# Head norms of the mixer: the sums of squares as eight 512-column matmuls into one 8-row tile, three of them in the last recurrence

## The chip, the cores and the metric

The kernel runs on one core of one Trainium2 chip, as one launch. The metric is the time of one execution on the device, in microseconds (us): the median of three runs. One further execution is recorded by the profiler, and all rows in this document come from such records.

## The reference, cut to what matters

The program is a decoder trunk of two layers on 512 tokens. A layer begins with a "mixer": four heads of differential attention and four heads of a gated delta rule (a recurrence over chunks of 64 tokens). Each head gives a vector of 128 numbers for each token. Each of the eight vectors is normalized on its own, and the recurrent ones are multiplied by a gate:

```
o = rms_norm(o, subln_g) * (1.0 - lam_init)                     # attention, each head over its 128 numbers
o = rms_norm(o, norm_g) * jax.nn.silu(z.reshape(...))           # delta rule, each head over its 128 numbers
h = h + jnp.concatenate([o_da, o_gdn], axis=-1) @ w_out[i]
```

with `rms_norm(x, g) = x * rsqrt(mean(x * x) + 1e-6) * g`. The product with `w_out` (1024 x 1024) follows, then a mixture of experts, which is much the larger part of the layer.

## The kernel before, in words

Everything lies transposed: features on the 128 partitions, tokens along the columns. `mixt` is [128, 8, 512]: eight heads (0 to 3 attention, 4 to 7 delta rule), 128 features on the partitions, 512 tokens. Each engine has its own instruction stream written out by hand, and the streams meet at counted semaphores. An engine runs its stream in order.

The mixer. `mixer` runs for t = 0 to 3 (128 tokens each, two chunks of 64) thirteen steps k. Steps 0 to 8 invert the chunk matrices (`invert`, L1122), steps 9 to 12 are the recurrence (`recur`), and in every step `attend` puts a piece of the attention of head t, so that both fill each other's gaps. In the recurrence, for chunk c = 2t and c = 2t + 1: `values_of(c)` (PE, L1204) multiplies the state; VectorE subtracts it from `u_sb` (`new_values`, L1655, which gives semaphore step_vn); `state_of(c)` (PE, L1213, 4 products of 128 columns) makes the update, which VectorE adds to the state (`new_state`, L1661); `output_of(c)` (PE, L1224 and L1225, 8 products of 64 columns) makes the output of the chunk, which ScalarE copies to `mixt` (L699). ScalarE copies the transposed w to `pw` (L691) before the first `values_of` of a t. In the attention, unit u is one block of 128 queries: scores (L1038), exponentials on ScalarE (L705), weights on VectorE (L1575 to L1584), `turn(u)` (transposes on PE, L1046), the copy `turned(u)` on ScalarE (L718), `weighted(u)` (PE, L1055), and for a whole head the copy `head_out` to `mixt` (L711).

The norms, after the mixer. ScalarE squares the eight heads into `sq_mix` (L448). PE sums over the partitions with the squares as the stationary operand and one column of ones as the moving one: `norm_sums`, 8 heads x 4 token blocks = 32 products of one column (L408), into 32 columns of bank 4. ScalarE takes the roots (L439), VectorE the reciprocals (L444), and PE spreads each over 128 partitions again (`norm_spread`, L432, 4 products of 128 columns for each head, into banks 5 and 6 in turn). VectorE scales head by head (L1702), then multiplies heads 4 to 7 by the gate `gzt` (L1707), and ScalarE and VectorE split the result into `act_hi` (L770) and `act_lo` (L452), which the product with `w_out` takes (`slab_product`, L385 to L387: three products of 512 columns for each of 8 input blocks, and so for each of 8 output slabs; its first slab waits for each `act_lo` block). The matrices here are plain fp32 except in `slab_product`, where they are fp32r (one pass). The profile records each plain fp32 product as two MATMUL records.

PE's own line for this tail:

```
mixer(invert, recur, attend)
weighted(H * NT - 1)
pe.wait_ge(S["at_oc"], H)
norm_sums(pe, "mix", 2 * H, sq_mix)
norm_spread(pe, "mix", 2 * H)
```

## Time and profile before

| | us |
|---|---|
| median of three runs (lowest, highest) | 3712.5 (3712.1, 3715.87) |
| profiled execution, its own time | 3716.72 |
| its span, first to last instruction | 3714.9 |

PE is busy for 95% of the span, VectorE for 75%, ScalarE for 41%, GpSimd for 34%. The stage of this change stands in the span twice, once in each layer: from 387.3 to 417.0 us and from 2230.7 to 2260.3 us. To read it one wants the chain of work that ended last in that stretch, the waits, and TensorE's granted clock, which has two levels here: 1.00 (2.4 GHz) and 0.50 (1.2 GHz).

### The profile page before, as it was taken

What the parts mean: (1) busy time and instruction counts of PE and PEld (TensorE: products, weight loads), DVE (VectorE), ACT (ScalarE), POOL (GpSimd) and SP (SyncE); (2) the same over time, 40 slices, a digit from 0 to 9 for tenths busy, and PEclk for the clock granted to TensorE, in tenths of its full rate; (3) what the DMA queues carried; (4) which work ended last, traced back from release to release, by engine and by line L of the source; (5) the groups of instructions that cost most, each with busy time, mean ns of one, the idle gap of its engine ahead of it and who ended that gap; (6) DMA issues with size and microseconds to landing.
All of it is one profiled execution on the core that took longest, in us unless ns stands there. A gap on an engine that the chain in (4) does not pass through costs nothing.

```text
span 3714.9 us, 60532 instructions
## 1 busy us (share of the span) xinstructions
PE 3515.7 (95%) x20002; PEld 3316.9 (89%) x20002; DVE 2780.4 (75%) x5764; ACT 1522.7 (41%) x2306; POOL 1276.7 (34%) x1052
## 2 busy tenths in 40 slices
PE   7999999999998999999899899999999989999997
PEld 5877899999998999999778778999999989999996
DVE  6257478898886888888562664888988878888884
ACT  4334333336664333333333433333476633333333
POOL 0000001218774456665000000022277744565640
PEclk9999799999999999999999988999999999999998
DMA  3200144448889999999222002444588899999981
GB/s 131 80 24 1 46 139 147 145 161 291 299 298 354 370 368 375 371 380 359 92 76 80 7 1 68 139 145 148 179 291 301 298 355 383 367 377 371 367 325 61
DMA packets 266273, 814.24 MB, mean 219 GB/s; under 512 B 24816, under 2 KB 106992, under 8 KB 262512
## 3 DMA queue, kind: packets, MB, share of 16 engines
q1 hardware_dynamic: 92592, 339.05, 25.3%
q0 software_dynamic: 73728, 268.47, 19.2%
q10 hardware_dynamic: 99776, 204.50, 15.4%
q8 instruction: 94, 1.54, 0.2%
q14 instruction: 83, 0.68, 0.1%
HBM read 709.16 MB, written 102.76 MB: 219 GB/s over the span
## 4 chain that ended last, share of the span: by engine, by line
PE 63%; DMA 18%; DVE 10%; issue 5%; POOL 3%; ACT 1%; DVEq 1%; SPq 0%; ACTq 0%; POOLq 0%; PEldq 0%
PE bank L385 16%; PE bank L386 16%; PE bank L387 16%; DMA gath<-slabs,rows_of 10%; DMA gath<-u_rows,rows_of 6%; PE bank L1342 5%; POOL gath L537 2%; PE bank L1122 2%; DVE acc L1982 2%; PE bank L408 2%; DVE wlo L382 1%; PE bank L432 1%; DVE act_w L1943 1%; PE bank L1298 1%; PE bank L1225 1%
## 5 line engine op out<-in xcount | busy, mean ns | idle before, releaser
L382 DVE TENSOR_TENSOR wlo<-raw,whi 128x1024 fp32r<-128x1024 f32 x636 | 803.1, 1263 | 410.1 <-ACT whi L375 377.8
L385 PE MATMUL bank<-act_hi,whi 128*128 128x384 f32 (+1 forms) x2944 | 1054.2, 358 | 22.0 <-DVE act_lo L452 13.7
L386 PE MATMUL bank<-act_lo,whi 128*128 128x384 f32 (+1 forms) x2944 | 1040.7, 354 | 0.0
L387 PE MATMUL bank<-act_hi,wlo 128*128 128x384 f32 (+1 forms) x2944 | 1040.3, 353 | 0.0
L375 ACT ACTIVATE whi<-raw 128x1024 fp32r<-128x1024 f32 x636 | 674.9, 1062 | 500.8 <-PE bank L387 460.0
L385 PE MATMUL bank<-w_hi,whi 128*128 128x384 f32 x2048 | 698.6, 341 | 54.9 <-DVE w_lo L1948 54.7
L386 PE MATMUL bank<-w_lo,whi 128*128 128x384 f32 x2048 | 692.9, 338 | 0.0
L387 PE MATMUL bank<-w_hi,wlo 128*128 128x384 f32 x2048 | 692.6, 338 | 0.0
L529 POOL TENSOR_TENSOR onehot<-onehot,cidx 128x800 f32<-128x800 f32 x56 | 124.0, 2244 | 1547.9 <-DVEq L1833 1547.9
L385 PEld LDWEIGHTS bank<-act_hi,whi 128*128 128x128 f32 x2944 | 558.3, 190 | 64.2 <-issue 13.4
L537 POOL DMA_INDIRECT gath<-slabs,rows_of x256 | 489.1, 1910 | 298.8 <-DVE acc L1982 257.5
L387 PEld LDWEIGHTS bank<-act_hi,wlo 128*128 128x128 f32 x2944 | 557.5, 189 | 36.4
L386 PEld LDWEIGHTS bank<-act_lo,whi 128*128 128x128 f32 x2944 | 558.5, 190 | 34.9
L537 POOL DMA_INDIRECT gath<-u_rows,rows_of x256 | 349.6, 1366 | 459.9 <-DVE gath L1916 348.9
L385 PEld LDWEIGHTS bank<-w_hi,whi 128*128 128x128 f32 x2048 | 391.2, 191 | 65.5 <-issue 65.0
L1982 DVE SCALAR_TENSOR_TENSOR acc<-gath,hi_spare,acc 128x1024 f32<-128x1024 f32 x256 | 324.5, 1280 | 106.5 <-DMA gath<-slabs,rows_of 106.3
L386 PEld LDWEIGHTS bank<-w_lo,whi 128*128 128x128 f32 x2048 | 391.8, 191 | 0.0
L387 PEld LDWEIGHTS bank<-w_hi,wlo 128*128 128x128 f32 x2048 | 391.1, 191 | 0.0
L811 ACT ACTIVATE hst<-bank 128x384 f32<-128x384 f32 x256 | 125.6, 491 | 586.7 <-PE bank L387 568.7
L1916 DVE SCALAR_TENSOR_TENSOR gath<-gath,lo_spare 128x1024 f32<-128x1024 f32 x256 | 309.1, 1218 | 60.8 <-DMA gath<-u_rows,rows_of 59.6
L897 ACT ACTIVATE w_hi<-act_w 128x384 fp32r<-128x384 f32 x256 | 133.1, 520 | 310.6 <-DVE act_w L1943 308.7
L553 POOL TENSOR_SCALAR hot<-consts,n_cols 128x128 f32<-128x128 f32 x288 | 226.1, 793 | 0.0
(293 smaller groups left out, 3862.8 us busy)
## 6 DMA issues: line engine op xcount, KB each, us to landing
raw<-slabs SPq DMA_DIRECT2D x636, 512.0 KB
hidden_dram<-hst ACTq DMA_DIRECT2D x256, 192.0 KB
gates_dram<-stage ACTq DMA_DIRECT2D x24, 2048.0 KB
h_sb<-hidden_dram ACTq DMA_DIRECT2D x64, 768.0 KB
g_sb<-gates_dram ACTq DMA_DIRECT2D x32, 1536.0 KB
gath<-u_rows,rows_of POOLq DMA_INDIRECT x256
gath<-slabs,rows_of POOLq DMA_INDIRECT x256
res<-x_t SPq DMA_DIRECT2D x1, 2048.0 KB, 9.1
```

What stands on the lines that cost most here:

```text
L375: nc.scalar.activation(whi[k][:], raw[k][:], ACT.Copy).then_inc(s_slab_hi, 1)
L382: nc.vector.tensor_tensor(wlo[k][:], raw[k][:], whi[k][:].bitcast(F32), ALU.subtract).then_inc(s_slab_lo, 1)
L385: nc.tensor.matmul(out, a_hi, b_hi, start=first, stop=False)
L386: nc.tensor.matmul(out, a_hi, b_lo, start=False, stop=False)
L387: return nc.tensor.matmul(out, a_lo, b_hi, start=False, stop=last)
L537: nc.gpsimd.indirect_dma_start(gath[n % GR][:].rearrange("p k c -> p (k c)"), None, table, bass.IndirectOffsetOnAxis(ap=rows_of[:, n // P, ...
L553: last = nc.gpsimd.tensor_scalar(hot1[b % 2][:, tok, :], iota, n1_cols[b % 2][:, tok:tok + 1], None, ALU.is_equal)
L811: nc.scalar.activation(hst[k][:], bank[2 + k % 2][:, 0:TD], ACT.Gelu).then_inc(S["u_gelu"], 1)
L897: nc.scalar.activation(w_hi[r][:], act_w[r % 2][:, 0:TD], ACT.Copy).then_inc(S["w_hi_ready"], 1)
L1342: last = nc.tensor.matmul(heads(4 + i % 4)[:, s, :], hot1[b % 2][:, tok, :], hot2[b % 2][:, tok, :], start=True, stop=True)
L1916: V.scalar_tensor_tensor(gath[r][:], gath[r][:], 1.0, x_nat, ALU.mult, ALU.mult, accum_out=col).then_inc(S["gath_used"], 1)
L1982: V.scalar_tensor_tensor(acc[r % 2][:], gath[r][:], col, acc[r % 2][:], ALU.mult, ALU.add).then_inc(S["gath_used"], 1)
```

## The change

1. The sums. A new function `mix_sums` turns the operands round: the stationary operand is a slice of 8 columns of the constants with a one in column g and zeros elsewhere, the moving operand are the 512 columns of a head's squares. Head g's sums land in row g of one [8, 512] tile in bank 2, and the eight products add up in it (32 one-column products before, 8 of 512 columns now).
2. Their places. The sums of attention heads 0, 1 and 2 are issued by PE in the last recurrence (t = 3, steps 9, 10, 11); those of heads 4 to 7 and of head 3 after `weighted(15)`. ScalarE squares heads 0, 1, 2 in steps 6, 7, 8, head 4 in step 12, heads 5 to 7 and head 3 at the end, into parts of tiles no longer needed (`daq`, `gqt`, `dak`).
3. The roots. ScalarE takes them on the [8, 512] tile into `std8`, PE turns that with four small transposes to [128, 32], and VectorE's reciprocal reads it from PSUM.
4. The gates. VectorE multiplies heads 4 to 7 by the gate before the scaling, as soon as their squares are taken, not behind it.
5. In the last t, `state_of` and `new_state` of the last chunk are left out (nobody reads that state); `output_of` gets the wait for step_vn for itself.
6. `warm(n)`: n products of 256 columns (fp32r) into bank 7, which nobody reads, on PE while it waits: 6 behind the sums, 4 behind the transposes, 10 behind the spread.

The diff, in the order `mix_sums`, ScalarE's stream (to the roots), PE's (from `k == 9` on), VectorE's (last piece):

```diff
+        def mix_sums(pe, first, last):
+            for i in range(first, last):
+                pe.wait_ge(S["sq_ready"], sq_seen("mix") + i + 1)
+                g = MIX_ORDER[i]
+                done = nc.tensor.matmul(bank[2][0:2 * H, :], consts[:, C_HOT + 7 - g:C_HOT + 15 - g], sq_mix[i],
+                                        start=i == 0, stop=i == 2 * H - 1)
+            if last == 2 * H:
+                done.then_inc(S["ss_ready"], 1)
...
                 def attend(t, k):
                     u = NT * t
                     last = t == NT - 1
+                    if last and k in (6, 7, 8):
+                        act.wait_ge(S["at_oc"], k - 5)
+                        mix_square(k - 6)
...
                     elif k == 12:
+                        if last:
+                            act.wait_ge(S["og_copied"], 2 * NT)
+                            mix_square(3)
                         turned(u + 3 if last else u + 2)
...
                 mixer(invert, recur, attend)
+                for i in range(4, 7):
+                    mix_square(i)
                 head_out(H - 1)
-
                 act.wait_ge(S["at_oc"], H)
-                act.wait_ge(S["og_copied"], 2 * NT)
-                act.wait_ge(S["step_state"], 2 * NT)
-                act_squares(act, mixt, 2 * H, sq_mix)
-                norm_std(act, "mix", 2 * H, 1.0 / P)
+                mix_square(2 * H - 1)
+                act.wait_ge(S["ss_ready"], nth("mix") + 1)
+                nc.scalar.activation(std8[:], bank[2][0:2 * H, :], ACT.Sqrt, bias=eps_col[0:2 * H],
+                                     scale=1.0 / P).then_inc(S["std_ready"], 1)
...
                     elif k == 9:
                         turn(u + 1)
+                        if last:
+                            mix_sums(pe, 0, 1)
                     elif k == 10 and last:
                         scores_of(u + 3)
                         weighted(u + 1)
+                        mix_sums(pe, 1, 2)
                     elif k == 11:
                         if last:
                             turn(u + 2)
+                            mix_sums(pe, 2, 3)
...
                     else:
-                        state_of(2 * t + 1)
+                        if more:
+                            state_of(2 * t + 1)
                         output_of(2 * t + 1)
...
                 weighted(H * NT - 1)
+                mix_sums(pe, 3, 2 * H)
...
+                def warm(n):
+                    for i in range(n):
+                        nc.tensor.matmul(bank[7][:, 0:2 * P], whi[S_OUT % RING][:, 0, :],
+                                         whi[S_OUT % RING][:, 2:4, :], start=True, stop=True)
+                pe.wait_ge(s_slab_hi, S_OUT + 1)
+                warm(6)
+                pe.wait_ge(S["std_ready"], nth("mix") + 1)
                 pe.wait_ge(S["at_oc"], H)
-                norm_sums(pe, "mix", 2 * H, sq_mix)
+                for t in range(NT):
+                    last = nc.tensor.transpose(bank[4][:, 8 * t:8 * t + 8], std8[:, t * P:(t + 1) * P],
+                                               ident[0:2 * H, 0:2 * H])
+                last.then_inc(S["std_turned"], 1)
+                warm(4)
                 norm_spread(pe, "mix", 2 * H)
+                warm(10)
...
-                norm_rs(dve, "mix", 2 * H)
+                for j in range(H):
+                    dve.wait_ge(S["sq_ready"], sq_seen("mix") + 3 + j + 1)
+                    V.tensor_tensor(mixt[:, H + j, :], mixt[:, H + j, :], gzt[:, j, :], ALU.mult).then_inc(S["mix_z"], 1)
+                dve.wait_ge(S["std_turned"], 1)
+                V.reciprocal(rs[:, 0:2 * H * NT], bank[4][:, 0:2 * H * NT]).then_inc(S["rs_ready"], 1)
```

PE's stream in steps 11 and 12 of the last t, before (L1046 is `turn(14)`, L1213 `state_of(7)`, L1224 and L1225 `output_of(7)`, L1055 `weighted(14)`; the numbers behind the names tell buffers apart):

```order
L1225 MATMUL bank3<-intra1_115,u_sb_113 128x64
L1046 MATMUL bank5<-consts_50,at_w_100 128x128 x3
L1213 MATMUL bank7<-u_sb_113,kdec1_110 128x128 x4
L1224 MATMUL bank3<-qdec1_112,state1_98 128x64
```

and now (L1252, L1068, L1251 are the same three lines, L446 is `mix_sums`):

```order
L1252 MATMUL bank3<-intra1_115,u_sb_113 128x64
L1068 MATMUL bank5<-consts_50,at_w_100 128x128 x3
L446 MATMUL bank2<-daq_80,consts_50 8x512
L1251 MATMUL bank3<-qdec1_112,state1_98 128x64
```

The product of the last state update has gone and the sum of head 2 stands in its place. PE's stream from `weighted(15)` to the first product with `w_out`, before:

```order
L1055 MATMUL bank4<-at_wt_101,v_nat_73 128x128 x4
L408 MATMUL bank4<-consts_50,sq_mix_116 128x1 x32
L432 MATMUL bank5<-consts_50,rs_53 128x128 x4
```

and now (L1077 is `weighted(15)`, L1292 `warm`, L1299 the transposes of the roots, L436 the spread, L389 the first product):

```order
L1077 MATMUL bank4<-at_wt_101,v_nat_73 128x128 x4
L446 MATMUL bank2<-gqt_77,consts_50 8x512 x4
L446 MATMUL bank2<-dak_81,consts_50 8x512
L1292 MATMUL bank7<-whi0_59 128x256 x6
L1299 MATMUL bank4<-consts_50,std8_116 128x8 x4
L1292 MATMUL bank7<-whi0_59 128x256 x4
L436 MATMUL bank5<-consts_50,rs_53 128x128 x4
```

The 32 one-column products have become five of 512 columns here, and ten unread ones and four transposes stand between them and the spread. ScalarE's stream in steps 6 to 9 of the last t, now (L719 exponentials of unit 13, L674 the scaling of `kdec`, L737 a square, L705 the copy of w to `pw2`, which in the kernel before stands right behind `kdec`):

```order
L737 ACTIVATE daq_80<-mixt_76 128x512
L719 ACTIVATE at_s_99,at_c_102<-at_s_99,at_c_102 128x256 x2
L674 ACTIVATE kdec1_110<-kn_nat_71,gsm_84 128x128 x4
L737 ACTIVATE daq_80<-mixt_76 128x512 x2
L705 ACTIVATE pw2_75<-bank7 128x512
```

One square stands ahead of the exponentials and two ahead of the copy on which the recurrence's first product waits.

## Rows read from the trace of the kernel before

**Rows 1.** The page: the span, and busy time by engine.

```profile
span 3714.9 us, 60532 instructions
PE 3515.7 (95%) x20002; PEld 3316.9 (89%) x20002; DVE 2780.4 (75%) x5764; ACT 1522.7 (41%) x2306; POOL 1276.7 (34%) x1052
```

**Rows 2.** The chain that ended last, layer 1: start us, us, what.

```profile
384.54 2.09 PE bank L1055 x8
386.65 0.60 ACT mixt L711
...
388.06 13.80 PE bank L408 x64
401.88 0.29 ACT cols L439
402.20 0.36 DVE rs L444
402.61 10.50 PE bank L432 x64
...
413.79 2.49 DVE mixt L1707 x4
416.28 0.61 DVE act_lo L452
...
417.03 0.77 PE bank L385
```

**Rows 3.** Windows of layer 1: us, engines' busy us (records), PE clock, DMA share, GB/s.

```profile
99.00:104.00 5.00, 5.00 (x23) 1.87 (x22) 3.88 (x5) 1.96 (x3) 0.00 (x0) 1.00 0.28 105
370.90:373.80 2.90, 2.90 (x18) 2.36 (x17) 2.77 (x6) 0.00 (x0) 0.00 (x0) 1.00 0.00 0
374.10:381.30 7.20, 7.20 (x27) 5.77 (x25) 3.57 (x11) 2.19 (x6) 0.00 (x0) 0.50 0.00 1
388.00:400.00 12.00, 11.95 (x57) 11.98 (x57) 0.00 (x0) 4.83 (x8) 0.00 (x0) 0.50 0.01 1
408.30:413.00 4.70, 4.70 (x40) 4.46 (x38) 3.57 (x5) 1.26 (x2) 0.00 (x0) 1.00 0.00 0
415.10:417.00 1.90, 0.00 (x0) 0.00 (x1) 1.90 (x4) 1.90 (x5) 0.00 (x0) 0.50 0.00 0
417.00:421.50 4.50, 4.47 (x11) 3.53 (x12) 4.50 (x8) 0.89 (x1) 0.00 (x0) 0.50 0.01 4
```

**Rows 4.** Timeline, PE: start us, us, engine, line, form, count [idle before].

```profile
98.93 0.40 PE L386 MATMUL bank<-act_lo,wba_hi 128*8 128x512 f32 x1
363.02 1.06 PE L1122 MATMUL bank<-inv_b,kbg 128*128 128x128 f32 x8
370.88 0.43 PE L1224 MATMUL bank<-qdec,state 128*128 128x64 f32 x2
374.42 2.08 PE L1213 MATMUL bank<-u_sb,kdec 64*128 64x128 f32 x8
377.66 0.69 PE L1224 MATMUL bank<-qdec,state 128*128 128x64 f32 x2
2260.32 0.47 PE L385 MATMUL bank<-act_hi,whi 128*128 128x512 f32 x1 [3.94 <-DVE act_lo L452]
```

**Rows 5.** Timeline, ScalarE and VectorE: start us, us, engine, line, form [idle before].

```profile
364.12 0.60 ACT L691 ACTIVATE pw<-bank 128x512 f32<-128x512 f32 x1 [0.34 <-PE bank L1122]
387.28 4.26 ACT L448 ACTIVATE sq_mix<-mixt 128x512 f32<-128x512 f32 x8
402.20 0.35 DVE L444 RECIPROCAL rs<-cols 128x32 f32<-128x32 f32 x1 [22.97 <-ACT cols L439]
404.72 0.75 DVE L1702 SCALAR_TENSOR_TENSOR mixt<-mixt,lam,bank 128x512 f32<-128x512 f32 x1 [2.17 <-PE bank L432]
413.13 0.75 DVE L1702 SCALAR_TENSOR_TENSOR mixt<-mixt,par,bank 128x512 f32<-128x512 f32 x1 [0.24 <-PE bank L432]
```

**Rows 6.** One line's instructions, both layers: duration ns (min, median, max).

```profile
L1002 PE MATMUL bank<-consts,ba_t x8: 202/202/223, 126.1 to 1963.5; 8*128 8x8 f32 x8
```

More of the change, by code:

```diff
@@ L96 @@
 C_EPS = C_POS + NC
-NCONST = C_EPS + 2
+C_HOT = C_EPS + 2
+NCONST = C_HOT + 16
 Q_MIX, Q_FFN, Q_PLE, Q_FIN = 0, 8, 16, 24
@@ L224, in trunk @@
         m3 = [gates_at + (16 * 16 + 80) * 4]
-        sq_mix = place("sq_mix", [P, 2 * H, T], F32, m3)
+        std8 = place("std8", [2 * H, T], F32, m3)
+        sq_mix = [daq[:, 0, :], daq[:, 1, :], daq[:, 2, :], gqt[:, 0, :], gqt[:, 1, :], gqt[:, 2, :], gqt[:, 3, :],
+                  dak[:, 0, :]]
+        MIX_ORDER = (0, 1, 2, H, H + 1, H + 2, H + 3, 3)
         m = [arena]
@@ L333, in trunk @@
             rhs_ready kdec_ready qdec_ready uw_ready uw_copied step_v step_vn step_s step_o step_state og_copied state_zero
-            mix_scaled mix_z mix_ready wout_added q_hi_ready q_lo_ready rstd_copied qt_scaled wq_evac subk_ready
+            mix_z std_turned wout_added q_hi_ready q_lo_ready rstd_copied qt_scaled wq_evac subk_ready
             score_ready score_read tk_dve tk_act selt_ready selt_copied
@@ L719, in turned, with mix_square @@
                                          ACT.Copy).then_inc(S["at_trc"], 1)
+                def mix_square(i):
+                    nc.scalar.activation(sq_mix[i], mixt[:, MIX_ORDER[i], :], ACT.Square).then_inc(S["sq_ready"], 1)
                 def attend(t, k):
@@ L1219, in output_of @@
                         pe.wait_ge(S["qdec_ready"], t + 1)
+                        pe.wait_ge(S["step_vn"], c + 1)
                         if c > 0:
@@ L1682, in recur @@
                             setup(t + 1, "pow_n")
-                        new_state(2 * t + 1)
+                        if more:
+                            new_state(2 * t + 1)
                 setup(0, "arg_t")
@@ L1696, in _ @@
                 mixer(invert, recur, attend)
-                norm_rs(dve, "mix", 2 * H)
+                for j in range(H):
[3 more added lines that the diff above has]
+                V.reciprocal(rs[:, 0:2 * H * NT], bank[4][:, 0:2 * H * NT]).then_inc(S["rs_ready"], 1)
                 for j in range(2 * H):
                     dve.wait_ge(S["rstd_bc"], bc_seen("mix") + j + 1)
+                    if j >= H:
+                        dve.wait_ge(S["mix_z"], j - H + 1)
                     gain = lam[:, 70:71] if j < H else par[:, Q_GDN:Q_GDN + 1]
@@ L1703, in _ @@
                     i.then_inc(S["norm_used"], 1)
-                for j in range(2 * H):
-                    dve.wait_ge(S["norm_used"], used_seen("mix") + j + 1)
-                    if j >= H:
-                        V.tensor_tensor(mixt[:, j, :], mixt[:, j, :], gzt[:, j - H, :], ALU.mult).then_inc(S["mix_ready"], 1)
                 act_low(dve, mixt, KD)
@@ L2068, in constants @@
     c[:, C_EPS] = EPS
+    c[:, C_HOT + 7] = 1
     return c
```

5 lines of the change are left out of this document (1 added, 4 removed).

## The prediction

> **What bounds the kernel now.** I looked first at the page: PE is busy for 95% of the span [rows 1]. A busy PE can still be a PE with nothing useful to do, so the second view was the chain of work that ended last, in the stretch of the norms. There the steps stand one behind the other with no cover: `weighted(15)` 2.09 us, the copy of head 3, the 32 one-column products 13.80 us, the roots, the reciprocals, the spread 10.50 us, the gates 2.49 us, the first `act_lo`, the first product with `w_out` at 417.03 us [rows 2]. From the end of the copy to that product it is 29.8 us, twice in the span. Nobody works beside it: VectorE has been idle for 22.97 us when it takes the reciprocals [rows 5], and the DMA engines are at 0.00 to 0.01 [rows 3]. So what is saved here is saved in full, as long as the next stage is bound by PE. The third view, windows with the granted clock, says at what clock this runs: 0.50 from 374.1 us through the whole sums, 1.00 in the second half of the spread, then 0.50 again for the first products (11 records in 4.5 us) [rows 3]. Half of the stage's length is the clock.
>
> **What the clock follows.** While `output_of(6)` ran (370.9 to 373.8 us), PE was busy for 2.90 of 2.90 us at 1.00, and then the clock fell [rows 3]. Those are products of 64 columns. Under one-column products it stayed at 0.50 for 12 us of a PE that was busy throughout; under the 512-column products it came back after 4.5 us. From about 98.9 us on 24 products have a stationary operand of 8 columns only and 512 moving ones (one of them stands in [rows 4]); they lie in a stretch at 1.00, 23 records in 5.00 us [rows 3]. [...]
>
> **The price of a new sum.** No plain fp32 product of 128 rows and 512 columns is in the trace. From one side: four fp32 products of 128 columns are 8 records in 1.06 us at 1.00 [rows 4], of which the last record's tail is about 0.2, so 0.21 us each; four times the columns give 0.86 us, and 1.71 us at 0.50. From the other side: two records at the pace of the 8-column products, 0.22 us, would be 0.43 us. I take 0.86, since the 128-column rows are plain fp32 as the new sums are and those 8-column ones are not.
>
> **The walk, at the times of layer 1.** I follow the streams from 361 us with the durations of before and full clock.
> - ScalarE: a square costs 4.26 / 8 = 0.53 us [rows 5]. One lands ahead of the exponentials of unit 13 (a gap of 0.3 us takes most, 0.15 late), two between `kdec` and the copy of w. That copy starts at 364.9 instead of 364.12 [rows 5], and the recurrence's first product with it: 0.75 us late.
> - PE: the sum of head 0 stands ahead of `state_of(6)`, which waited for VectorE anyway; that makes 0.97 late. The sum of head 1 stands ahead of `values_of(7)`, which waited too: 1.08 late, at 371.0. `output_of(6)` takes 2.9 us (0.365 for each of 8 pairs of records, from its 0.43 rows with their tails), `turn(14)` 0.3, the sum of head 2 0.86; `state_of(7)` is gone (2.0 us at half clock [rows 4]). `output_of(7)` starts at 376.0.
> - From here before ran at 0.50. At 1.00: `output_of(7)` 2.9 us instead of 4.9 (0.62 a pair, the 0.69 rows), `weighted(14)` 0.64, `turn(15)` 0.43, the copy 0.60 and two hand-overs; the weights of unit 15 are no longer behind `new_state(7)` on VectorE and are there in time. `weighted(15)` starts at 380.9 instead of 384.54 and streams for 0.86 us. The squares of heads 4 to 6 (ScalarE, from 380.8) and 3 (after its copy, done at 383.5) stay ahead of the sums that need them. Five sums, 4.3 us and a tail of 0.15: done at 386.2, where before it was 401.86 [rows 2].
> - Roots: 512 columns from PSUM are the 0.60 us of the head copy [rows 2] where 32 columns were 0.29; `warm(6)` (6 x 0.11) ends before them. The four transposes have a twin, the transposes of `ba_t` with the same 8 rows, 202 ns each and overlapped [rows 6]: 0.4 us and a hand-over. Reciprocal 0.35, with `warm(4)` beside it. The spread starts at 387.7 instead of 402.61.
> - First scaling 1.2 us behind that at 1.00 (2.11 at 0.50 [rows 2, 5]), the last one seven steps of 1.0 us later (that is PE's pace at 1.00: 40 records in 4.70 us, 8 a head [rows 3]): 395.8 instead of 413.13.
> - The gates (2.49 us) have moved to where VectorE was idle. They cost nothing while that idle time is there (from 402.20 - 22.97 = 379.2 us on [rows 5]; in the walk 8 us are left of it); without it, 2.5 us. `act_lo` follows the last scaling after 0.7 us, the first product 0.83 us later: 397.35 instead of 417.03. That is 19.7 us.
> - The first products: 11 records at 0.43 instead of 0.22 us in layer 1 [rows 3], 2.2 us; 8 in layer 2 (started at 2260.32 [rows 4] with the clock still up, which fell and came back), 1.6 us. `warm(10)`, 1.1 us, fills the 1.7 us between the spread and them, so the clock has no reason to fall, and it delays nothing.
>
> Sum: 19.7 + 2.2 = 21.9 us in layer 1, 19.7 + 1.6 = 21.3 in layer 2, whose start stands in the same place of its stage: 43.2 us if the clock holds all the way.
>
> **What the clock takes back.** It may not. `output_of(7)` is again 2.9 us of 64-column products, now between the sum of head 2 and `weighted(14)`, and the same stretch with the same neighbours fell in one place and not in the other in this very trace: where in it the chip looks decides. A fall at about 381 us, behind `output_of(7)`, would make `weighted(15)` and three of the five sums run at half clock: 0.86 + 3 x 0.86, about 3.4 us. I take one such fall in the two layers: 43.2 - 3.4 = 39.8 us. Against the profiled execution (3716.72 us, its span and 1.8 us around it) that is 3676.9; that execution is 4.2 us above the median, which the position of the clock's falls explains as well as anything, so from the median 3712.5 I expect **3672.7 us**.
>
> The Trainium skill, in "TensorE: Matmul & The Clock Gate", section "HAM oscillation — how this bites in real kernels", puts the loss of the clock down to idle gaps of PE between bursts of products. The trace disagrees: the fall at 374 us came out of 2.90 us of unbroken work. By the page's rule there is no fall at all after the change, and the sum would be 43.2 us.
>
> **The rivals.**
> 1. The clock holds in both layers: 43.2 us, 3669.3. For it: there are 2.6 us of 512-column work more in the recurrence, and the page's rule above. Against: the fall out of a busy PE. Chance 0.28.
> 2. It falls early in both, as before at 374 us. Then `output_of(6)`'s end, the sum of head 2 and everything to `weighted(15)` run at 0.50, the sums begin at 387.4 at 0.50 and bring the clock back after 3.7 us: done at 393.7, 7.5 us later than in the walk. Gain 14.4 + 13.8 = 28.2 us, 3684.3. For it: same place, same products. Against: two sums more right around them. Chance 0.2.
> 3. The clock doesn't come back under the sums either. Five at 1.71 us: done at 396.1, `warm(6)` and `warm(4)` (0.21 each now) delay the rest by about 1 us, the spread starts 3.8 us earlier than before and runs as before; with the gates gone 2.4 us more, and up to 2.2 for the first products. 6.2 to 8.4 us a layer, 14.6 in all: 3697.9. Against it: the stretch from 99 us at 1.00. Chance 0.09.
> 4. The time is given back behind the stage, by slabs that arrive late: within 7 us of before, 3709. The DMA engines are idle here and four slabs lie ready; nothing speaks for it. Chance 0.04.
> 5. Slower: a 512-column sum costs much more than 0.86 us, for instance because fp32 squares can't be streamed at that pace. Eight of them stand on the path in each layer; the gain of 21.6 us is gone when each costs 2.7 us more, 3.6 in all. At 4 us each it would be 8 x 3.15 - 21.6 = 3.6 us a layer, 3719.7. Against: no fp32 row has a pace above 0.21 us for 128 columns. Chance 0.03.
>
> My forecast, one or a few short falls, 36 to 41 us: 0.36.
>
> **The numbers.** Rival 1 to rival 2 is 3669 to 3684, which holds 0.84. The unknown costs (the roots, hand-overs, the sum from 0.43 us up: eight sums at 0.43 less would be 3.4 us a layer) and the spread of a few us by the clock's falls elsewhere widen that to 3665 to 3689. What a measurement of this kernel tells from no change is about 0.2%, 7.4 us: faster by more than that 0.93 (all but rivals 4 and 5), the same 0.04, slower 0.03.
>
> **What would show it.** In the changed profile: two records of about 0.43 us for each sum at 1.00; PE's sums done about 5.3 us behind the start of `weighted(15)`; VectorE's idle time ahead of the reciprocals under 5 us; the spread at 1.00 from its first record; the first product 9.7 us behind the start of the spread, and its records at 0.22 us from the first on; the stage (start of the head copy to first product) about 15 us instead of 30.4. Wrong would be: sums at 1.71 us, a spread at 0.50 (rival 3), a clock of 0.50 from 374 us on (rival 2), or a PE that waits for slabs in the first products (rival 4).

## The result, and the profile after

| | before | after |
|---|---|---|
| median, us (lowest to highest), 4 executions each | 3712.3 (3700.56 to 3715.87) | 3657.25 (3654.71 to 3662.85) |
| profiled execution: its time, its span | 3716.72, 3714.9 | 3655.65, 3653.8 |

The ratio is 0.9869, 95% interval 0.9849 to 0.9889: 55 us faster. The forecast was 3672.7, its range began at 3665.0, so the change gave more than the range allowed. A second comparison of the same two kernels gave 0.9855 (0.9824 to 0.9885).

The page of the changed kernel, for [rows 1]:

```profile
span 3653.8 us, 60398 instructions
PE 3480.2 (95%) x19938; PEld 3274.3 (90%) x19938; DVE 2780.2 (76%) x5756; ACT 1522.4 (42%) x2306; POOL 1285.0 (35%) x1052
```

PE (TensorE's matmuls) has a share of 95% in both; it was busy for 35.5 us less, but the page does not say where in the span the 61 us went. The chain that ended last in layer 1 does, for [rows 2] (start us, us, what):

```profile
384.63 0.61 ACT at_wt L732
...
385.27 2.07 PE bank L1077 x8
387.35 5.81 PE bank L446 x10
393.16 0.91 PE bank L1292 x6
394.07 0.35 PE bank L1299 x4
394.41 0.67 PE bank L1292 x4
395.08 7.84 PE bank L436 x64
...
402.95 0.75 DVE mixt L1752
403.69 0.61 DVE act_lo L466
...
404.44 0.47 PE bank L389
```

The 13.80 us of one-column sums are 5.81 us now (five of the eight sums; the other three lie in the recurrence), and ScalarE's copy of head 3 is off the chain, since PE has other heads' sums to do meanwhile. The spread takes 7.84 us where it took 10.50. The gates (2.49 us) are gone from between the last scaling and the first `act_lo`. The windows with the granted clock, for [rows 3]:

```profile
375.40:378.30 2.90, 2.90 (x17) 2.37 (x16) 2.84 (x5) 0.00 (x0) 0.00 (x0) 1.00 0.00 0
379.80:382.70 2.90, 2.90 (x18) 2.36 (x17) 1.56 (x4) 1.01 (x4) 0.00 (x0) 1.00 0.00 0
384.00:390.70 6.70, 6.01 (x16) 2.57 (x15) 2.45 (x4) 4.66 (x7) 0.00 (x0) 0.54 0.01 2
391.00:394.00 3.00, 3.00 (x13) 1.05 (x10) 0.00 (x0) 0.68 (x1) 0.00 (x0) 1.00 0.00 0
394.90:400.80 5.90, 5.90 (x50) 5.54 (x48) 3.74 (x5) 2.52 (x4) 0.00 (x0) 1.00 0.00 1
405.00:411.00 6.00, 6.00 (x28) 4.95 (x27) 5.34 (x8) 1.04 (x2) 0.00 (x0) 1.00 0.03 8
```

Both `output_of` pass at 1.00; then the clock falls for 6.8 us (383.35 to 390.17 us by the trace's clock record), over the end of `weighted(14)`, `turn(15)`, `weighted(15)` and the first one and a half of the last five sums, and is back at 1.00 before the sums end. Spread and first products are at 1.00 throughout. The same in PE's timeline, for [rows 4]:

```profile
369.91 1.03 PE L446 MATMUL bank<-daq,consts 128*8 128x512 f32 x2
370.87 1.04 PE L1239 MATMUL bank<-u_sb,kdec 64*128 64x128 f32 x7
...
385.27 2.07 PE L1077 MATMUL bank<-at_wt,v_nat 128*128 128x128 f32 x8 [0.69 <-ACT at_wt L732]
387.28 5.02 PE L446 MATMUL bank<-gqt,consts 128*8 128x512 f32 x8
392.13 1.02 PE L446 MATMUL bank<-dak,consts 128*8 128x512 f32 x2
...
394.00 0.42 PE L1299 MATMUL bank<-consts,std 8*128 8x8 f32 x4
```

A sum is two records and takes 370.87 - 369.91 = 0.96 us at full clock, which is close to the 1.06 us, tail included, of the four fp32 products with 128 standing and 128 moving columns in [rows 4]: the same number of moving columns in all. ScalarE and VectorE, for [rows 5]:

```profile
393.19 0.68 ACT L788 ACTIVATE std<-bank,consts 8x512 f32<-8x512 f32 x1 [3.25 <-PE bank L446]
383.86 0.69 DVE L1744 TENSOR_TENSOR mixt<-mixt,gzt 128x512 f32<-128x512 f32 x1 [1.35 <-ACT gqt L737]
385.77 1.90 DVE L1744 TENSOR_TENSOR mixt<-mixt,gzt 128x512 f32<-128x512 f32 x3 [1.22 <-ACT gqt L737]
394.45 0.36 DVE L1746 RECIPROCAL rs<-bank 128x32 f32<-128x32 f32 x1 [6.78 <-PE bank L1299]
```

The gates lie where VectorE idled, and 6.78 us of that idle time are left.

**The stage measured as a whole.** From the start of the last copy of w to the first addition of the product with `w_out`, read in the same way from every trace (a0 and a1 are runs told of below; "half" is the time at clock 0.50 within it):

```
us                     w copy->   head copy  spread->   product->  whole   half
                       head copy  ->spread   product    addition
before        layer 1    22.54      15.95      14.42      8.02     60.93   41.0
before        layer 2    22.62      15.95      14.34      7.39     60.30   37.5
after         layer 1    19.49       7.53       9.52      5.77     42.32    6.8
after         layer 2    19.46       7.55       9.53      5.72     42.26    6.8
a0 (again)    layer 1    18.24       5.90       9.52      5.76     39.42    0
```

So the stage gave 18.6 and 18.0 us, 36.6 in all. These two traces are typical: in the 16 layers of the eight kernels that have the old stage (before, b0 to b4, d1, d2) it took 57.4 to 61.1 us, 59.7 in the mean; in the six layers of after, a0 and a6 it took 39.4 to 42.3, 41.3 in the mean. That is 36.8 us for two layers. The two spans differ by 61.1 us. Of the other 24.5 most lies where the diff changes no instruction: the expert stages, from the first to the last `w_hi` of a layer, took 572.1 and 575.7 us before and 566.1 and 564.2 after, 17.5 us less. The experiments follow both leads.

### The profile page after: what moved, and what is told of

It is laid out like the page before. It is cut to its first block, busy times and chain, and to the rows that moved or that the text cites. A ratio compares the mean times of both kernels' runs of the same rounds, so it can differ in the third digit from the quotient of the medians.

```text
span 3653.8 us, 60398 instructions
## 1 busy us (share of the span) xinstructions
PE 3480.2 (95%) x19938; PEld 3274.3 (90%) x19938; DVE 2780.2 (76%) x5756; ACT 1522.4 (42%) x2306; POOL 1285.0 (35%) x1052
## 4 chain that ended last, share of the span: by engine, by line
PE 68%; DMA 14%; DVE 9%; issue 4%; POOL 3%; ACT 1%; DVEq 1%; SPq 0%; ACTq 0%; POOLq 0%; PEldq 0%
PE bank L389 18%; PE bank L390 18%; PE bank L391 18%; DMA gath<-slabs,rows_of 8%; DMA gath<-u_rows,rows_of 6%; PE bank L1385 5%; POOL gath L551 3%; PE bank L1148 2%; DVE acc L2028 1%; DVE wlo L386 1%; PE bank L436 1%; PE bank L412 1%; PE bank L1341 1%; DVE act_w L1989 1%; DVE w_lo L1994 1%
## 5 line engine op out<-in xcount | busy, mean ns | idle before, releaser
L389 PE MATMUL bank<-act_hi,whi 128*128 128x384 f32 (+1 forms) x2944 | 1052.0, 357 | 12.6 <-DVE act_lo L466 6.2
L389 PE MATMUL bank<-w_hi,whi 128*128 128x384 f32 x2048 | 697.0, 340 | 41.7 <-DVE w_lo L1994 41.7
L389 PEld LDWEIGHTS bank<-act_hi,whi 128*128 128x128 f32 x2944 | 557.1, 189 | 54.2 <-issue 6.2
L551 POOL DMA_INDIRECT gath<-slabs,rows_of x256 | 499.4, 1951 | 277.8 <-DVE acc L2028 238.2
L389 PEld LDWEIGHTS bank<-w_hi,whi 128*128 128x128 f32 x2048 | 390.8, 191 | 49.3 <-issue 48.4
L1962 DVE SCALAR_TENSOR_TENSOR gath<-gath,lo_spare 128x1024 f32<-128x1024 f32 x256 | 309.3, 1219 | 50.1 <-DMA gath<-u_rows,rows_of 49.9
```

The source lines that it names most:

```text
L389: nc.tensor.matmul(out, a_hi, b_hi, start=first, stop=False)
L551: nc.gpsimd.indirect_dma_start(gath[n % GR][:].rearrange("p k c -> p (k c)"), None, table, bass.IndirectOffsetOnAxis(ap=rows_of[:, n // P, ...
L1962: V.scalar_tensor_tensor(gath[r][:], gath[r][:], 1.0, x_nat, ALU.mult, ALU.mult, accum_out=col).then_inc(S["gath_used"], 1)
```

## The experiments

Labels that begin with b or d are edits of the kernel before, those with a or c of the changed one. Ratios are to the kernel before, run on the same chip in turn.

### Before again, and the constants' width alone

```diff
-NCONST = C_EPS + 2
+NCONST = C_EPS + 2 + 16
```

> The kernel before, unchanged, profiled again beside the others. The profile of after has 24 us less than mine of before outside the norm stage (in the first three recurrences and in the expert stage whose DMA engines are full). Theory A (those 24 us differ from execution to execution: where the clock falls in the recurrences, and how fast the full DMA engines deliver): this execution shows the last recurrence with its norms (copy of w of t = 3 to the first addition of the product with w_out) again at 60 to 61 us in each layer, but the recurrences before it and the expert stage (first to last w_hi, 572 and 576 us in the first profile) other than the first profile by several us, and the span may be anywhere from 3699 to 3715. Theory B (they come from the change, by its place in memory or its time): this execution shows the expert stage at 572 to 576 us and the span at 3711 or more.

> The kernel before with only the 16 more columns of constants, which moves every tile behind them by 64 bytes. Theory A (the shift does nothing): ratio to before 1.000 within 0.002, expert stage as in the run of before beside it within a few us. Theory B (the shift makes the expert stage faster): expert stage 564 to 566 us as in the profile of after, against 572 to 576, and the time about 17 us lower.

> The changed kernel, profiled again. If the fall of the clock behind the last output product is a matter of where in the stretch the chip looks, as I predicted (one of two layers), it is there in some layers and missing in others: last recurrence with norms 42.3 us with a fall, about 39 without. If it is inherent, both layers show 42.3 and 6.8 us at half clock again. The rest of the span differs by several us from 3653.8 - 84.6 by theory A, by under 3 by theory B.

b0, unchanged: 0.9995 (0.9976 to 1.0015), expert stages 570.9 and 573.9 us. b1, which only makes the array of constants 16 columns wider, as the change does: 0.9979 (0.9956 to 1.0002), expert stages 565.7 and 562.9. a0, the changed kernel again: 0.9855 (0.9824 to 0.9885), 566.4 and 566.5. The total of b1 is not told apart from no change, but its expert stages are those of the changed kernel (565.7 and 562.9 us, as theory B had it, though the time went down by 8 us and not by 17). The tiles in SBUF are packed one behind the other, so 16 columns of 4 bytes move every later tile by 64 bytes.

### Which array's place it is

b2 moves the tiles in SBUF behind the constants by 64 bytes, and nothing else:

```diff
+        at[0] += 64
         par = place("par", [P, NPAR], F32)
```

b3 makes only the array in DRAM wider, and loads its old columns:

```diff
-            sp.dma_start(consts[:], consts_d).then_inc(consts_loaded, 16)
+            sp.dma_start(consts[:], consts_d[:, 0:NCONST]).then_inc(consts_loaded, 16)
...
-    c = np.zeros((P, NCONST), np.float32)
+    c = np.zeros((P, NCONST + 16), np.float32)
```

b4 moves only the late tiles, those of the expert stage (`gath`, `h_sb`, `g_sb0`):

```diff
-        late = max(late, m[0])
+        late = max(late, m[0]) + 64
```

> The kernel before with every tile behind the constants moved by 64 bytes in SBUF, and nothing else (the constants stay as they are, in SBUF and in DRAM). The run with 16 more columns of constants had an expert stage of 565.7 and 562.9 us against 570.9 and 573.9 in the kernel before beside it, with 92% of the gathered 4096-byte packets at 159 ns instead of 55%. Theory C (the place of the tiles in SBUF decides): expert stage 563 to 567 us and about 92% at 159 ns again, time about 15 us below before. Theory D (the place of the inputs in DRAM decides, since the constants are one of the input arrays): 571 to 576 us and about 55%, time as before.

> The kernel before with 16 unread columns more in the constants' array in DRAM, and SBUF as it was. The opposite of the run before: theory C gives 571 to 576 us and 55% of the gathered packets at 159 ns, theory D 563 to 567 us and 92%.

> The kernel before with only the tiles of the expert stage's loads (h_sb, g_sb0, gath and the two behind them) moved by 64 bytes, from 64 over a multiple of 128 to a multiple of 128; raw and all else stay on multiples of 128. Theory E (a transfer into rows that start 64 bytes off a multiple of 128 takes longer, and in the kernel before gath and h_sb do): expert stage 563 to 567 us, gathered packets about 92% at 159 ns, time 12 to 17 us below before. Theory F (the place of raw, or of the tiles that VectorE and ScalarE work on, decides): 571 to 576 us as before, and 55%.

b2 is faster, 0.9947 (0.9927 to 0.9967); b3 0.9983 (0.9971 to 0.9995); b4 0.9976 (0.9954 to 0.9997). The interval of b2 lies just below that of b3, and that of b4 overlaps both. b3 leaves SBUF as it was, and its interval stays below 1.000 all the same; so a total some 6 us lower shows nothing here. I therefore read the transfers themselves: the records of the 4096-byte packets of the indirect gathers within the expert stage (22,600 to 22,700 in each layer; the shares are those of layer 1, layer 2 lies within 4 points of them), against the place of `gath`, `h_sb` and `g_sb0`, as what it leaves over a multiple of 256 bytes:

```
kernel   place of gath   packets at 159 ns   expert stages, us
before        192               53%            572.1   575.7
b0            192               55%            570.9   573.9
b3            192               53%            569.9   575.0
d2            192               49%            574.0   568.4
b1              0               92%            565.7   562.9
b2              0               92%            567.0   569.1
b4              0               94%            567.1   575.0
after           0               92%            566.1   564.2
a0              0               92%            566.4   566.5
d1             64               83%            573.2   567.6
a6             64               84%            567.2   567.2
c2            128               86%            572.6   563.3
c1              0               92%            586.2   565.8
```

The other packets take 160 to 168 ns mostly. The share follows the place of these tiles in SBUF and nothing else that was moved: not the array in DRAM (b3). The difference is a few ns a packet: the mean of a layer's packets is 168.2 to 170.4 ns in the four kernels at 192 and 166.6 to 168.8 in b1, b2, b4, after and a0, about 1% apart and overlapping. The windows of the expert stage show what this meets, of before, of b2 and of after in turn (us; busy us and instructions of PE, PEld, VectorE, ScalarE, GpSimd; clock; DMA share; GB/s):

```profile
1212.50:1784.60 572.10, 544.79 (x3060) 539.26 (x3060) 487.04 (x619) 201.62 (x262) 311.55 (x176) 0.98 0.96 362
3055.70:3631.40 575.70, 545.45 (x3059) 540.17 (x3058) 487.21 (x619) 202.13 (x263) 318.65 (x176) 0.98 0.96 359
```

```profile
1211.40:1778.40 567.00, 543.41 (x3060) 537.12 (x3059) 487.32 (x619) 202.12 (x263) 311.94 (x176) 0.98 0.96 365
3038.50:3607.60 569.10, 542.29 (x3059) 534.03 (x3058) 487.26 (x620) 199.81 (x262) 310.38 (x176) 0.99 0.96 364
```

```profile
1197.10:1763.20 566.10, 543.25 (x3063) 539.26 (x3062) 487.29 (x619) 201.50 (x263) 323.19 (x176) 0.98 0.96 366
3007.10:3571.30 564.20, 542.96 (x3058) 539.26 (x3057) 487.77 (x619) 201.31 (x263) 316.10 (x176) 0.98 0.96 367
```

PE and VectorE do the same work in nearly the same busy time (PE within 3.2 us, VectorE within 0.8). The DMA engines are busy for 96% of it and move 359 to 362 GB/s in the one, 364 to 367 in the others, so I read the stage as one that lasts as long as its bytes; PE is busy for 95% of it too, by its modelled records. Who waits for them stands in the groups of the page (busy us, mean ns, idle us before and its releaser), of before and of b1:

```profile
L1982 DVE SCALAR_TENSOR_TENSOR acc<-gath,hi_spare,acc 128x1024 f32<-128x1024 f32 x256 | 324.5, 1280 | 106.5 <-DMA gath<-slabs,rows_of 106.3
L1916 DVE SCALAR_TENSOR_TENSOR gath<-gath,lo_spare 128x1024 f32<-128x1024 f32 x256 | 309.1, 1218 | 60.8 <-DMA gath<-u_rows,rows_of 59.6
```

```profile
L1982 DVE SCALAR_TENSOR_TENSOR acc<-gath,hi_spare,acc 128x1024 f32<-128x1024 f32 x256 | 324.6, 1280 | 96.6 <-DMA gath<-slabs,rows_of 95.9
L1916 DVE SCALAR_TENSOR_TENSOR gath<-gath,lo_spare 128x1024 f32<-128x1024 f32 x256 | 309.0, 1217 | 49.5 <-DMA gath<-u_rows,rows_of 47.5
```

VectorE's own instructions keep their 1280 and 1218 ns; its idle time ahead of them, nearly all of it a wait for gathered rows, is 21 us shorter.

### The tiles at other places

d1 moves all tiles by 128 bytes (`at[0] += 128` ahead of `par`). a6 is the changed kernel with 64 bytes more, 128 in all (the same line with 64). d2 moves all tiles by 64 and the late ones by 256:

```diff
+        at[0] += 64
         par = place("par", [P, NPAR], F32)
...
-        late = max(late, m[0])
+        late = max(late, m[0]) + 192
```

> The kernel before with all tiles behind the constants moved by 128 bytes: each keeps its remainder to 128 (raw 0, gath 64) and gets the other one to 256 (raw 0 instead of 128, gath 64 instead of 192). The changed kernel with that same place kept its fast expert stage (567.2 us twice), with 84% of the gathered packets at 159 ns. Theory G (the remainder to 256 or more decides, or any move from the old place): 565 to 568 us, about 84% at 159 ns. Theory E (the remainder to 128 decides, and the changed kernel's fast stage has another cause): 570 to 576 us and 55%.

> The kernel before with raw, the split weights and all tiles up to the late ones moved by 64 bytes, and gath, h_sb and g_sb0 by 256, so that those keep every remainder up to 256 that they had. If the place of the gathered and late tiles decides (which the run with only them moved says of the packets): 570 to 576 us and 55% at 159 ns. If raw and the rest have a share of their own: 565 to 570 us.

> The changed kernel with all tiles behind the constants moved by 64 bytes more, so that every tile has the remainder to 128 that it had before the change. If 64 bytes of remainder to 128 in the gathered tiles are the cause: expert stage back at 569 to 576 us, the time 12 to 17 us above the changed kernel (3663 to 3670 against 3650 to 3657 for the changed kernel in its two jobs). If it was something else about the first 64 bytes (remainder to 256, distance between tiles): expert stage 563 to 567 us and no difference.

d2, which moves everything but keeps the late tiles' remainder at 192, is as before: 0.9993 (0.9977 to 1.0010), 49% of the packets at 159 ns. For the packets this shows that these tiles count and not the others, `raw` with the weights among them. d1 0.9977 (0.9954 to 1.0000) and a6 0.9899 (0.9868 to 0.9930), both at remainder 64, lie between in their packets (83 and 84%).

In a single stage's time the place isn't seen safely: stages at one remainder differ by up to 8 us among themselves (b4: 567.1 and 575.0, where 563 to 567 were expected of both; d2: 574.0 and 568.4, where 570 to 576 were). The two stages of b4 are 1142.1 us together and those of d2 1142.4, so of the late tiles alone the stage's time shows nothing; all tiles moved together give 1128.6 (b1) and 1136.1 (b2) against 1142.4 to 1147.8 in the four kernels at 192. In sight of all kernels the difference is plain: of the 22 stages at 0, the changed kernels' included, 20 lie between 562.9 and 569.1 us (the others are b4's 575.0 and c1's 586.2), and of the eight at 192 seven lie between 569.9 and 575.7. By their means, 572.5 us over the eight stages at 192 (before, b0, b3, d2) and 567.8 over the six of b1, b2 and b4 at 0, it is 5 us a stage; against the 565.8 of after and a0 it is 7. The changed kernel was not run with these tiles at 192, so its own share of this is taken from the others.

### The parts of the change: form and places of the sums

a5 has the sums in their old form, all behind `weighted(15)`, and with them the roots on 32 columns and no transposes; the rest is the changed kernel:

```diff
...
-                mix_sums(pe, 3, 2 * H)
+                for i in range(2 * H):
+                    pe.wait_ge(S["sq_ready"], sq_seen("mix") + i + 1)
+                    g = MIX_ORDER[i]
+                    for t in range(NT):
+                        last = nc.tensor.matmul(bank[2][:, t * 2 * H + g:t * 2 * H + g + 1],
+                                                sq_mix[i][:, t * P:(t + 1) * P], one_col, start=True, stop=True)
...
```

a2 has the new form, but no sum in the recurrence:

```diff
-                            mix_sums(pe, 0, 1)
...
-                        mix_sums(pe, 1, 2)
...
-                            mix_sums(pe, 2, 3)
...
-                mix_sums(pe, 3, 2 * H)
+                mix_sums(pe, 0, 2 * H)
```

> The changed kernel with the 32 one-column products back (behind the last attention product, in bank 2, with the roots on 32 columns and no transposes); places of the squares, gates, the missing state update and the warm products stay. If the sums' form is what brings the gain: the clock falls under the one-column products (at 0.50 from within 7 us of their start), they take 10 to 13.8 us instead of 5, the spread runs half at 0.50, and the last recurrence with norms is 53 to 57 us a layer against 39.4 to 42.3, 25 to 30 us in the time. If the gain is mostly from gates, state and warm products, it stays under 47.

> The changed kernel with all eight sums behind the last attention product, none in the last recurrence; the squares stay where they are. If the three early sums do only their own work, the last recurrence with norms gets longer by what they cost behind it (3 x 0.96 us at full clock) less what they delay now (about 1.3 us of the recurrence, the sum of head 2 in full): about +1.0 us a layer. If they also hold up the clock, it falls at the output products as before, some 7 us earlier than now, and the stage gets 4 to 8 us longer a layer.

a5: 0.9922 (0.9897 to 0.9948), its stage 50.50 us in both layers with 23.9 us of half clock. PE's timeline of its layer 1, and three windows:

```profile
379.45 5.12 PE L1289 MATMUL bank<-consts,daq 128*128 128x1 f32 x24
384.43 6.97 PE L1289 MATMUL bank<-consts,gqt 128*128 128x1 f32 x32
391.26 1.84 PE L1289 MATMUL bank<-consts,dak 128*128 128x1 f32 x8
```

```profile
379.45:393.10 13.65, 13.65 (x66) 13.65 (x65) 0.53 (x1) 2.51 (x3) 0.00 (x0) 0.50 0.00 0
384.00:388.00 4.00, 4.00 (x20) 4.00 (x21) 0.00 (x0) 0.00 (x0) 0.00 (x0) 0.50 0.00 0
388.00:400.00 12.00, 12.00 (x68) 11.72 (x69) 2.77 (x5) 1.83 (x4) 0.00 (x0) 0.65 0.00 0
```

The one-column sums take 13.6 us (379.45 to 393.1), as was expected; the fall came earlier than expected, at 372.6 us under `output_of(7)`, and lasted through all of them. The stage was expected at 53 to 57 us, or under 47 if the form were not what brings the gain, and lies between. Against the changed kernel's 42.3 it is 8.2 us a layer longer, against a stage without a fall (39.4) 11.1: part of it is the products, part is the clock, which stayed at 0.50 while PE was busy with them. a5 also has all sums behind `weighted(15)`; a2, below, has them in the same places, so the form by itself (with the roots on 32 columns that go with it) is the difference between those two, 50.50 - 43.07 = 7.4 us a layer.

a2: 0.9895 (0.9875 to 0.9916), its stage 43.06 and 43.07 us, with 6.8 us of half clock like the changed kernel's 42.3. The early places are worth 0.8 us a layer: without the three sums in it, the stretch up to the head copy is 0.8 us shorter (18.62 against 19.46), and that from there to the spread 1.6 longer (9.15 against 7.55). PE is nearly always busy in the recurrence too, so about half of what is saved behind it is paid back in it. (A fall of 6.8 us lies in both.)

### The state update, the gates, the unread products

a3 keeps `state_of` and, in the same way, `new_state` of the last chunk:

```diff
-                        if more:
-                            state_of(2 * t + 1)
+                        state_of(2 * t + 1)
```

a4 has the gates behind the scaling, as before (and no longer behind the squares):

```diff
...
+                for j in range(H):
+                    dve.wait_ge(S["norm_used"], used_seen("mix") + H + j + 1)
+                    V.tensor_tensor(mixt[:, H + j, :], mixt[:, H + j, :], gzt[:, j, :], ALU.mult).then_inc(S["mix_z"], 1)
                 act_low(dve, mixt, KD)
```

a1 leaves out the products that nobody reads:

```diff
-                warm(6)
...
-                warm(4)
...
-                warm(10)
```

> The changed kernel with the last state update put back (PE's product of 128 columns x 4 and VectorE's addition in the last t). I costed its going at 2.0 us at half clock and about 1.0 at full clock on PE. If it is on the path with the clock up: last recurrence with norms about 1 us longer than in the changed kernel with the same fall (43.3 with a fall, 40.4 without). If VectorE's addition also delays the weights of unit 15: up to 2 us. If the products hold the clock up (they stand right ahead of the 64-column ones), the fall comes less often and it costs nothing.

> The changed kernel with the gates back behind the scaling. I costed them at 2.49 us a layer when they have no cover: last recurrence with norms 41.9 us without a fall of the clock and 44.8 with one. If PE's wait of 1.7 us more, to 4.2 us, also lets the clock fall (only 1.1 us of it is filled), the first products run at half clock and it is up to 2.2 us more in some layers.

> The changed kernel without its 20 unread products. If they hold the clock between the sums and the first product: without them the clock is lost there in some layers, the spread or the first products run at 0.50, and the stage (copy of w to first addition) is 2 to 6 us longer there, 43 to 48 us. If PE is left alone too shortly for that (1.3 us at the roots, 1.7 us ahead of the first product): no fall, the same 39.4 or 42.3 us within 0.5, or 0.3 us less since warm(6) ends behind the roots now.

a3: 0.9872 (0.9850 to 0.9893), stage 43.37 and 43.36 us with 6.8 us of half clock: the state update was worth 1.1 us a layer.

a4: 0.9915 (0.9884 to 0.9946), stage 43.45 (half clock 3.4) and 46.28 (10.2). From the spread to the first product it is 11.93 us instead of 9.52, and from there to the first addition 7.35 instead of 5.75. VectorE's timeline of its layer 1, and PE's first product:

```profile
394.40 1.64 DVE L1750 SCALAR_TENSOR_TENSOR mixt<-mixt,par,bank 128x512 f32<-128x512 f32 x2 [0.36 <-PE bank L436]
395.96 2.49 DVE L1754 TENSOR_TENSOR mixt<-mixt,gzt 128x512 f32<-128x512 f32 x4
398.37 4.90 DVE L466 TENSOR_TENSOR act_lo<-mixt,act_hi 128x512 fp32r<-128x512 f32 x8
...
399.20 0.47 PE L389 MATMUL bank<-act_hi,whi 128*128 128x512 f32 x1 [2.75 <-DVE act_lo L466]
```

The gates cost 2.4 us by themselves, and after PE has waited 2.75 us the clock falls to 0.50 at the first products (399.6 us), 1.6 more: 4.0 us a layer. In time, a4's median lies 6 us above those of a6 and c1, which ran beside it (3669.7 against 3663.5 and 3663.4); against a0, timed on another chip, its ratio asks for 22 us, but the two intervals touch.

a1: 0.9848 (0.9823 to 0.9873), stage 39.33 and 39.37 us, no half clock. PE's timeline of its layer 2, where it waits uncovered:

```profile
2200.47 0.38 PE L1298 MATMUL bank<-consts,std 8*128 8x8 f32 x4 [0.82 <-issue]
2201.30 8.05 PE L436 MATMUL bank<-consts,rs 128*128 128x128 f32 x64 [0.45 <-DVE rs L1743]
...
2210.88 0.47 PE L389 MATMUL bank<-act_hi,whi 128*128 128x512 f32 x1 [1.53 <-DVE act_lo L466]
```

The gaps of 0.82, 0.45 and 1.53 us bring no fall; the next window of its trace says so:

```profile
2210.90:2215.00 4.10, 4.10 (x18) 3.39 (x19) 4.10 (x8) 0.85 (x1) 0.00 (x0) 1.00 0.00 0
```

The unread products do nothing that these runs can measure. In a4 the gap was longer and the clock fell in spite of `warm(10)`; whether more of them would have held it there was not tested.

### One sum more inside a gap, and both leads together

c1 puts head 4's sum ahead of `weighted(15)`, where PE waits 0.69 us for ScalarE's copy in the changed kernel. c2 is c1 with all tiles 64 bytes further and the late ones another 64.

```diff
+                mix_sums(pe, 3, 4)
                 weighted(H * NT - 1)
-                mix_sums(pe, 3, 2 * H)
+                mix_sums(pe, 4, 2 * H)
```

> The changed kernel with the sum of head 4 issued between the transposes of unit 15 and its product, where PE waits 0.7 us for ScalarE's copy. The sum takes 0.96 us at full clock: at least 0.7 us of it is covered, so the stage is 0.6 to 0.8 us shorter with the clock up. With the gap filled the clock has less reason to fall behind the last output products: if it holds, the stage is 38.8 us in both layers instead of 42.3 with a fall.

> The changed kernel with the sum of head 4 in the gap ahead of the last attention product (38.76 us in both layers in its first run, no fall of the clock), and with raw and its neighbours as well as gath, h_sb and g_sb0 on multiples of 128 bytes. Stage 38.8 us in both layers, expert stage 563 to 567 us, time 3 to 5 us below the changed kernel, about 3648 (changed kernel 3650.8 and 3657.3 in its jobs); if only the remainder to 256 counts, gath at 128 over it may be slow or fast: 570 or more us would say that it counts.

c1's stage is 38.76 us in both layers and in c2 38.76 and 38.77, 3.5 below the changed kernel with its fall and 0.6 below it without; no fall in four layers. The kernels with the changed recurrence (after, a0, a1, a4, a6) had a fall in 5 of 10, and it began ahead of PE's wait of 0.69 us, so that filling the wait kept the clock up is not shown: four layers without a fall may be luck. c1 as a whole gave 0.9880 (0.9844 to 0.9916), with one expert stage of 586.2 us in its profile that I can't explain, c2 0.9855 (0.9826 to 0.9883). So neither is measurably below the changed kernel, though the stage is; c2 was expected at about 3648 us and had a median of 3656.8. 128 left over was not a better place than 0 either (86% of the packets against 92%).

## Why the forecast missed, step by step

**The step that failed** is a term that the prediction put at nothing without a reason: what the change does outside the mixer. Its sum of 43.2 - 3.4 = 39.8 us has the norm stage alone, and rival 4 looked only for time that is lost behind the stage. The 16 columns of constants with the standing one, in the diff from the start, move all tiles by 64 bytes, and the expert stages, which wait for their transfers, become 5 to 7 us shorter each by their means, 10 to 14 in all. That the place in SBUF does it is shown for the packets (b2, b3, b4 and d2 tell it from the rest). For the stage's time it rests on the means and on b1 and b2, which move all tiles; which of the tiles gives it stays open. Of its worth in the total b1 says 7.8 us (-0.7 to 16), b2 19.7 (12 to 27), b4 8.9 (1 to 17); but b3, with SBUF as it was, says 6.3 (2 to 11), so that b2 alone stands clear of it. The norms by themselves gave less than the 39.8 us forecast, so the place and the rest below make up more than the whole miss.

**The norm stage came out near the forecast.**
- The sum: 0.96 us, forecast 0.86. Two records at 0.48, and its length is near that of four products of 128 moving columns, as argued from [rows 4]. Rival 5 (4 us a sum) is out.
- Sums done 7.9 us behind the start of `weighted(15)` in layer 1 (393.16 - 385.27), forecast 5.3. The fall of the clock is in it; in layer 1 of a0, without a fall, it is 5.5.
- Roots 0.68 us (0.60), transposes 0.42 (0.4), reciprocal 0.36 (0.35).
- VectorE's idle time ahead of the reciprocals 6.78 us, where I wanted under 5: with the fall the sums come later (4.44 us in layer 1 of a0, without it). The gates were covered, as forecast.
- Spread at 1.00 from its first record; first product 9.52 us behind the spread's start, forecast 9.7. First products at 1.00, 28 records in 6.00 us.
- Head copy to first product 17.05 us with the fall and 15.42 without (a0), forecast 15.
- The state update 1.1 us (a3, with a fall in both), where the walk took 2.0 out at half clock.
- The clock: a fall behind `output_of(7)` was forecast in one layer of two, at 3.4 us. It was there in both layers of the changed kernel's profile, and in 5 of the 10 layers in a0, a1, a4, a6 and it, as well as in all four of a2 and a3. It costs 42.3 - 39.4 = 2.9 us. Rival 2 (a fall at the first `output_of`) and rival 3 (no return under the sums) did not happen, and rival 1 did in a1.
- The parts, each taken out alone: form of the sums 7.4 us a layer, their places 0.8, gates 4.0, state update 1.1, unread products nothing. That is 13.3 of 18.4. What is left has the places of ScalarE's squares in it, which were not run by themselves.

With two falls the prediction's own sum would be 43.2 - 6.8 = 36.4 us. The stage gave 36.6, less the two squares that stand ahead of the copy of w and so ahead of this stage's start, 0.75 us a layer in the walk and not measured by itself: 35. The two sizes meet in part by luck, since a fall cost 2.9 us and not 3.4; with that the sum is 37.4, some 2 us too much.

**What is left.** 55 us were measured; 35 in the norms and 10 to 14 by place leave 6 to 10. Two things lie there. In the spans compared, the half clock outside the norm stages is 196 us before (177 in b0) and 173 after (168 in a0). And medians move: that of before was 3705.2, 3709.9, 3702.2 and 3704.5 in the four later comparisons, against 3712.5 in the three executions that the forecast started from, and that of the changed kernel was 3657.3 and 3650.8. A start from 3705 would have lowered the forecast by 7 us in absolute time; the ratio it would have left as it is. Between the traces of b0 and after nearly all of it closes: of 50.1 us (3703.9 - 3653.8) the norm stages hold 33.8 and the expert stages 14.5, which leaves 1.8. Whether the remaining us of the medians are the clock in the recurrences or the measurement (each ratio is uncertain by 7 to 11 us) no run here settles.

The Trainium skill's rule that the prediction weighed ("TensorE: Matmul & The Clock Gate", "HAM oscillation — how this bites in real kernels") puts the loss down to idle gaps. In a4 the clock fell right behind a gap of 2.75 us, lengthened by the gates, which agrees with it. But it also fell behind `output_of(7)`, after products that kept PE busy for 2.90 of 2.90 us by its records, and in a5 it stayed at 0.50 under one-column products on a busy PE; there the trace disagrees. In this kernel the clock was lost behind a wait in one case and behind busy stretches of 64-column products in the other.

## What to carry to other kernels

A change that widens a tile moves all tiles allocated behind it: keep the tiles that a DMA-bound stage fills at fixed places, or run the move alone before crediting the edit. Sums over partitions are dear with one moving column (7 to 11 us a layer here) and cheap with the data moving (0.96 us for 512 columns). A step that moves into a stretch where its engine is busy already gains little beyond the gap it fills (0.8 us a layer here for three sums of 0.96 us).

## What the runs showed of the hardware

- A 4096-byte packet of a gather took 159 ns in 92 to 94% of cases (layer 1) when the tiles of its stage left 0 over a multiple of 256 bytes in SBUF, in 83 to 86% at 64 and 128, in 49 to 55% at 192, and 160 to 168 ns mostly otherwise. The mean packet differed by about 1% only. What in the chip does this was not found.
- The rate of that stage was 359 to 363 GB/s in before and b3 and 364 to 368 in b1, b2 and after, at a DMA share of 0.96 to 0.97. It did not always go with the place: b4's second stage, at 0, had 360, and d2's second, at 192, had 364.
- The clock came back from 0.50 to 1.00 while five sums with 8 standing and 512 moving columns ran in plain fp32 (they began at 387.28 us, it rose at 390.17). Under one-column products of a PE as busy it did not: 12 us at 0.50 in [rows 3], and all of their 13.6 us in a5.
